# Moving the tensors in on-chip memory: weights at multiples of 1 KB, activation regions 96, 160 and 288 bytes past one

## What is computed

```python
h = rmsnorm(x, g_pre[i])
(gq, gk, gv, ga, gz, dq, dk, dv, iq, ik, iw, dz, xq, xz, gates) = split_cols(h @ w_in[i])
...
merged = (s_gla * (y_gla @ w_gla_out[i]) + s_dsa * (y_dsa @ w_dsa_out[i])
          + s_mem * (y_mem @ w_x_out[i]))
x = x + rmsnorm(merged @ w_o[i], g_post[i])
# second block, for each of two layers
mix = jnp.concatenate([main, mo], axis=-1) @ w_out[l]
x = x + rmsnorm_2(mix, g_mix_post[l])
x = x + rmsnorm_2(swiglu(rmsnorm_2(x, g_ffn_pre[l]), w_ffn_in[l], w_ffn_out[l]), g_ffn_post[l])
```

## The kernel before

| tensor or region | bytes past a multiple of 1 KB |
|---|---|
| raw, whi, wlo, K | 128 |
| H, XR, R | 192 |
| V / gpost, small | 768 / 192 |

## Time and profile before

### The profile page before, as it was taken

The page is one execution under the profiler, slowest core; times in us unless marked ns, Lnnn a source line. Parts: engine busy times, 40 slices in busy tenths (PEclk is TensorE's granted clock), DMA queues, the critical chain, the costliest instruction groups (busy, mean ns, idle before and its releaser), DMA issues.

```text
span 2001.5 us, 32809 instructions
## 1 busy us (share of the span) xinstructions
PE 1968.7 (98%) x13488; PEld 1781.3 (89%) x13488; DVE 1145.0 (57%) x1595; ACT 932.6 (47%) x1647; POOL 145.5 (7%) x149
## 2 busy tenths in 40 slices
PE   8999999999999999999999999999999999999998
PEld 6798888877889778888999899999988799999998
DVE  3375347465343233353353999972377659999523
ACT  4443142355433342355454755652258856565422
POOL 0000000000000000000000233300000003333000
PEclk9999999999999999999999999999999999999999
DMA  6521122211334123332212233332231113223331
GB/s 179 146 85 64 43 84 84 85 64 59 111 112 162 63 106 105 106 116 89 81 48 80 77 125 106 106 126 95 97 116 43 64 64 116 106 106 106 127 106 64
DMA packets 29824, 191.24 MB, mean 96 GB/s; under 512 B 3689, under 2 KB 4841, under 8 KB 8562
## 3 DMA queue, kind: packets, MB, share of 16 engines
q1 hardware_dynamic: 26562, 178.58, 25.4%
q0 software_dynamic: 3120, 10.62, 2.0%
HBM read 185.38 MB, written 3.67 MB: 94 GB/s over the span
## 4 chain that ended last, share of the span: by engine, by line
PE 90%; DVE 5%; ACT 3%; issue 1%; DMA 1%; SPq 0%; DVEq 0%; ACTq 0%
PE PS L561 21%; PE PS L563 20%; PE PS L562 20%; PE PS L1034 6%; PE PS L1036 6%; PE PS L1035 6%; DVE wlo L2721 1%; ACT whi L1546 1%; PE PS L895 1%; PE PS L714 1%; PE PS L731 1%; PE PS L1152 1%; PE PS L917 1%; PE PS L851 1%; PE PS L1344 1%
## 5 line engine op out<-in xcount | busy, mean ns | idle before, releaser
L2323 DVE TENSOR_TENSOR wlo<-raw,whi 128x2048 fp32r<-128x2048 f32 (+2 forms) x117 | 264.9, 2264 | 375.3 <-ACT whi L1546 374.9
L1546 ACT ACTIVATE whi<-raw 128x2048 fp32r<-128x2048 f32 (+2 forms) x250 | 311.7, 1256 | 211.1 <-PE PS L563 190.7
L561 PE MATMUL PS<-hhi,whi 128*128 128x512 f32 (+1 forms) x768 | 313.2, 408 | 3.1 <-DVE hlo L2370 3.0
L563 PE MATMUL PS<-hhi,wlo 128*128 128x512 f32 (+1 forms) x768 | 302.7, 394 | 0.0
L562 PE MATMUL PS<-hlo,whi 128*128 128x512 f32 (+1 forms) x768 | 301.3, 392 | 0.0
L561 PE MATMUL PS<-whi,ahi 128*128 128x256 f32 x704 | 196.1, 279 | 0.0
L562 PE MATMUL PS<-wlo,ahi 128*128 128x256 f32 x704 | 196.1, 279 | 0.0
L563 PE MATMUL PS<-whi,alo 128*128 128x256 f32 x704 | 196.1, 278 | 0.0
L561 PEld LDWEIGHTS PS<-hhi,whi 128*128 128x128 f32 (+1 forms) x768 | 144.4, 188 | 40.7 <-DVE hlo L2370 5.4
L1034 PE MATMUL PS<-shi,whi 128*128 128x256 f32 x640 | 179.5, 280 | 0.9 <-DVE gated_ L2766 0.4
L1036 PE MATMUL PS<-shi,wlo 128*128 128x256 f32 x640 | 178.5, 279 | 0.0
(11 more groups left out here) (458 smaller groups left out, 4605.8 us busy)
## 6 DMA issues: line engine op xcount, KB each, us to landing
raw<-in_stream SPq DMA_DIRECT2D x165, 1024.0 KB, 4.8
gpost<-in_gposts POOLq DMA_DIRECT2D x5, 512.0 KB, 7.6
X<-in_x SPq DMA_DIRECT2D x4, 512.0 KB, 6.1
X<-in_x POOLq DMA_DIRECT2D x1, 2048.0 KB, 10.4
out<-X SPq DMA_DIRECT2D x4, 512.0 KB, 2.6
bias_line<-linet POOLq DMA_DIRECT2D x1, 1536.0 KB, 35.1
tbias<-bias_line POOLq DMA_DIRECT2D x1, 1024.0 KB, 7.5
memx<-in_mem POOLq DMA_DIRECT2D x1, 1024.0 KB, 5.4
```

The lines of the kernel that those rows point to most:

```text
L561: nc.tensor.matmul(out, lh, rh, start=(k == 0), stop=False)
L563: return nc.tensor.matmul(out, ll, rh, start=False, stop=(k == n_k - 1))
L1546: return nc.scalar.activation(out_, in_, func, scale=scale)
L2323: V_.tensor_tensor(wlo[:, s % 2, :, cols_], raw[:, s % 2, :, cols_], whi[:, s % 2, :, cols_], ALU.subtract)\
```

## The change

The tensors are declared in another order, and padding is put between them. `K` comes first and is followed by 64 floats (256 bytes) of padding, so that `raw`, `whi` and `wlo` begin at multiples of 1 KB: 16,512 + 5,760 + 256 = 22,528. Before H stand 24 floats of padding (96 bytes), before XR 16 more (64 bytes), before R 32 more (128 bytes). `V`, `gpost` and `small` move behind R. Every engine's instructions are the same and in the same order; only their addresses differ.

| tensor or region | past a multiple of 1 KB before | after |
|---|---|---|
| raw, whi, wlo | 128 | 0 |
| K | 128 | 128 |
| H | 192 | 96 |
| XR | 192 | 160 |
| R | 192 | 288 |
| V | 768 | 288 |
| gpost, small | 192 | 736 |

```diff
--- before.py
+++ after.py
@@ -52,6 +52,10 @@
 
 
 MASK_COLS = (256, 384, 512)
+
+
+TO_KB = 64
+APART = 24
 
 
 TAKEN = -3.4e38
@@ -275,13 +279,12 @@
                 base.enter_context(nc.sbuf_tensor(name, [P, kbytes * 256], F32))
             return place, close
 
+        K = sb("K", [P, K_ALL])
+        sb("to_kb", [P, TO_KB])
         raw = sb("raw", [P, 2, KT, C])
         whi = sb("whi", [P, 2, KT, C], F32R)
         wlo = sb("wlo", [P, 2, KT, C], F32R)
-        K = sb("K", [P, K_ALL])
-        V = sb("V", [P, V_COLS])
-        gpost = sb("gpost", [P, D])
-        small = sb("small", [P, 512])
+        sb("apart", [P, APART])
 
 
 
@@ -302,6 +305,7 @@
 
 
 
+        sb("apart_x", [P, 16])
         place, close = region("XR", 16)
         X = place("X", 0, [P, NT, D])
         maskt = place("maskt", 0, [P, sum(MASK_COLS)])
@@ -313,6 +317,7 @@
         xpt = place("xpt", 8, [P, 2, 2, T])
         close()
 
+        sb("apart_r", [P, 32])
         place, close = region("R", 99)
 
         yhi = place("yhi", 0, [P, KT, T], F32R)
@@ -417,6 +422,10 @@
                     for i, half in enumerate(("hi", "lo")))
         sums = {name: place(name, 88 + 2 * j, [P, 4, P]) for j, name in enumerate(("T1", "T2", "T3", "T4a", "T4b"))}
         close()
+
+        V = sb("V", [P, V_COLS])
+        gpost = sb("gpost", [P, D])
+        small = sb("small", [P, 512])
 
         slg = [slg0, slg_first] + [slg0, slg1] * 5
         PS = ctx.enter_context(nc.psum_tensor("PS", [P, 8, 512], F32))
```

## The result

The changed kernel takes 2027.51 us (two runs, 2023.93 and 2031.1) against 1996.34: ratio 1.0139, 95% interval 1.0106 to 1.0171. It is slower, by less than 2%; I had forecast 1989 within 1950 to 2036. The profiled execution has a span of 2021.9 us against 2001.5.

A forecast was written before the change was run, and what follows sets the result against it. TensorE, with 90% of the chain of waits, was taken as the bound. Address effect 0 and redrawn rhythms 7.7 us saved: 2001.5 - 7.7 = 1993.8, less the span's 5.2 above the median, gave 1989, range 1950 to 2036.

The forecast's parts named there:

- TensorE's spacing: Time from one matmul's start to the next: 113.4 or 117.7 ns at 256 columns, 228.8 at 512.
- term for V, gpost, small or the loads: Small operands of VectorE and ScalarE taken at 0, bound 8 us either way; loads of raw 0.
- Two rhythms: TensorE's 256-column matmuls run at 113.4 or 117.7 ns in windows without a pause, nothing between.
- third rival: Activations off multiples of 64 bytes need one more read piece per matmul: 27.7 us, 2024, or 43 us, 2039; 18%.
- a rhythm is kept until the next pause: A pause lets TensorE's matmul stream fall into 113.4 or 117.7 ns; only pauses turn one into the other.
- I take the change of spacing by address as 0: Matmul spacing in TensorE: new addresses change it by 0, with ends of 127.9 us saved and 43 us lost.
- The 7.7 us that I took off for redrawn rhythms: 256-column matmuls: each stretch draws its rhythm anew, long share from 71% to 50%, 7.7 us saved.
- My own sign of being wrong altogether: In the changed kernel's profile, matmul spacings that are neither about 113.4 nor 117.7 ns.
- The first: Rival on TensorE's matmuls: distance matters, the new one leaves only the short rhythm; 31.9 us saved, 1964; 22%.
- The second: Rival on TensorE's matmuls: even the short rhythm holds a stumble that goes too; 80 us saved, 1916; 9%.

The follow-up runs named there:

- experiment 1: Changed kernel with H, XR and R all 64 bytes past a multiple of 1 KB, weights still on one: ratio to before 1.0005.
- experiment 10: Kernel before, with the 576 matmuls streaming yhi taking their stationary operand from yhi and ylo instead of whi and wlo: 2004.04 us.
- experiment 11: Kernel before, with the feed-forward's sums 128 bytes further on, so 192 instead of 64 from the weights modulo 256: ratio to before 1.0009.
- experiment 9: Changed kernel, with the 576 matmuls streaming yhi taking their stationary operand from yhi and ylo instead of whi and wlo: 2019.26 us.
- experiment 4: Changed kernel with H 128, XR 192 and R 256 bytes past a multiple of 1 KB, weights on one: ratio to before 1.0161.
- experiment 2: Changed kernel with everything 32 bytes further on, all distances between weights and regions kept: ratio to before 1.0150.

## Why the prediction was wrong

**What held.** TensorE's spacing was the only thing that the change could touch; no term for V, gpost, small or the loads was needed (experiment 1). Two rhythms exist at one set of addresses. Executions at distance 64 drew 113.4 or 117.8 anew each time: streamed weights past R had means of 115.8, 115.7, 114.5 and 116.7 ns in the kernel before, experiments 1, 10 and 11. The bounds held too: 28.0 us lie over the 27.7 of the third rival but under its 43.

**What I had too narrow: pauses.** I had written that a rhythm is kept until the next pause. In the kernel before it also changed without one:

```profile
602.02 0.28 PE L563 MATMUL PS<-cmhi,wlo 128*128 128x256 f32 x1
...
604.14 0.28 PE L563 MATMUL PS<-cmhi,wlo 128*128 128x256 f32 x1
...
604.50 0.28 PE L563 MATMUL PS<-whi,cmlo 128*128 128x256 f32 x1
...
606.88 0.28 PE L563 MATMUL PS<-whi,cmlo 128*128 128x256 f32 x1
```

Up to 604.14 there are 18 spacings of 117.8 ns, from 604.50 on 21 of 113.3. At 604.26 TensorE goes over from streaming activations to streaming weights, and all that stands between are spacings of 117, 123 and 119 ns. At 1332.5, where the output product of the feed-forward begins, it is the same, with spacings of 121 and 116 ns between. So a change of product can change the rhythm too.

**The step that failed** is "I take the change of spacing by address as 0". I concluded from one set of addresses with two rhythms that addresses don't decide. The rows could not bear that: all pairs of the kernel before lie 64 apart, so the trace held a single value of the one variable that mattered. Two rhythms at one distance say nothing about a third one at another distance. The measured term is +1.94 ns a matmul of 256 columns and +3.98 ns at 512 instead of 0, together 28.0 us. The 7.7 us that I took off for redrawn rhythms rested on draws that do happen at the distance 64, but in the changed kernel the rhythm of 113.4 isn't to be had in any long stretch. My own sign of being wrong altogether, spacings that are neither of the two, is met by the 120.0 and 118.3 ns of the windows above. The measured time lay inside my range only because I had kept wide bounds for other mechanisms.

**The rule** that I leaned on (the Trainium skill, SBUF — State Buffer, "Who interferes with whom": two read ports of TensorE, independent, and TensorE never waits) disagrees with experiments 9 and 10. A move of the stationary operand alone changes the spacing by 6 ns and by 2 ns. A disturbance by VectorE isn't seen here: in experiment 4, at distance 0 from R, streamed sums had 119.6 ns where VectorE was busy in 129.80 of 140 us (1720 to 1860), and streamed weights 120.0 where it was busy in 34.29 of 95.

**The rivals.** The first had the right variable with the wrong sign: the new distances are worse than 64, not better. The second (under 113 ns) never appeared at 256 columns, though at 512 columns a distance of 0 brings 227 to 228. The third had nearly the right time, 2024, and a wrong reason; experiments 2 and 4 refute it. Its test as I wrote it, "windows streaming activations stand at 122 or more while those streaming weights stay", fails as well: both kinds grew. That 28.0 us lie so near its price of 27.7 is luck. It had priced 15.3 us for streamed activations of 256 columns, 12.4 for 512 columns and nothing for streamed weights; measured are 4.3, 11.2 and 12.5. Only the term at 512 columns was near.

**What stays open.** Why the period is 256 bytes, and why the spacing is shortest at a distance of 0 with 512 columns and at 64 with streamed weights of 256, no run tells. Nor does one tell whether a stream meets its own stationary load or that of the next matmul. Distances between the multiples of 32 were not tried.

## What to carry to other kernels

In this kernel, which is bound by back-to-back fp32r matmuls, the distance modulo 256 bytes between streamed and stationary tensors was worth up to 1.6%, and an edit that adds a small tensor between large ones can change it unnoticed. One that moves all of them together does not (experiment 2). So note the addresses of the large operands beside each time, and hold the distance when declarations are moved. A trace in which a variable has one value is no evidence that the variable doesn't matter; one run with another value costs less than an argument. When one rival's time fits the result, test its reason all the same.

## What I had not expected of the hardware

Spacings of matmuls settle in rhythms that hold for over 100 us (1,079 matmuls at 117.7 ns in the earlier trace rows) and that depend on the pair's distance modulo 256 bytes: at 512 columns 226.8 to 234.2 ns, at 256 columns 113.4 to 120.1. No distance reached the columns at 2.4 GHz, 213.3 and 106.7. Between executions of the kernel before the granted clock over the span varied from 0.993 to 0.999; in the traces these are drops to half, to 1.2 GHz, of which the longest lasted 13.7 us (at 245.8 us in experiment 2).
